# A hybrid decoder step on one Trainium2 core: filler matmuls moved inside the paged-attention rounds

## The chip, the cores and the metric

The kernel runs on one core of one Trainium2 chip. Its time is the device time of one execution in microseconds (us), the median of several executions. TensorE (PE) does the matmuls and the transposes, VectorE (DVE) and ScalarE (ACT) empty the PSUM banks and prepare operands, GpSimd (POOL) and SyncE (SP) mostly issue DMAs.

## The reference

Two trunk layers of a decoder are computed for a prompt group of 1024 tokens and for a sample group of 8 sequences with 4 new tokens each (1056 columns in all). The change touches only layer 0, and of it the part in which the sample group attends to its paged cache. In short:

```python
past_k = cache_k[j, page_table].reshape(nb, -1, DA_HEADS, 2 * DA_DIM)   # 8 sequences x 16 pages of 128 tokens
past_v = cache_v[j, page_table].reshape(nb, -1, DA_HEADS, 2 * DA_DIM)
...
proj = u @ w_in                                    # gate_b, gate_c, xin, q, k, v
conv_y, conv_new = short_conv(gate_c * xin, conv_w, conv_buf)
y_conv = gate_b * conv_y
...
s = einsum('bqhcd,bkhcd->bhcqk', q, keys) * (DA_DIM ** -0.5)
p = softmax(where(mask, s, -inf))
w = p[:, :, 0] - lam * p[:, :, 1]
attn = einsum('bhqk,bkhe->bqhe', w, vals)
mixed = concatenate([y_conv, rmsnorm(attn, subln_g) * (1 - lam_init)]) @ w_out
```

The convolution branch needs gate_c, xin and gate_b for 512 channels, that is 4 groups of 128 channels with three projections each.

## The kernel before

Every weight is split into a high and a low fp16 part, so a projection of 128 output channels (a *visit*) is computed as three products for each of the 8 slices of the input. A visit has three *units*, one for each third of the 1056 columns (352 columns, one PSUM bank). A unit is 24 matmuls of 128x352 (L369), and is issued in two *halves* of 12. The high part of a weight is made by ACT (L326), the low part by DVE (L342). A unit is drained from its bank by ACT (L1482) or by DVE (L1541 and L1545 for xin, L1560 for gate_b). In this stage nearly all of these units use the single bank 7, so a unit cannot start before the one ahead of it is drained.

The sample attention (`pe_samples`, `act_samples`, `dve_samples`) runs in two rounds of 4 sequences. A round consists of:

- the *K phase*, 32 steps. A step transposes two pages of K on PE (L1910, 8 transposes, banks 4 and 5), ACT copies one bank out (L1979) and DVE the other (L2039), and PE computes the scores of the step before (L1898). The transposes of a step wait until the banks of the step before are copied.
- the *middle*, 4 steps: own scores (L1917, L1921), maxima on DVE (L2034 to L2047), exponentials on ACT (L1985, L1987), the combination of the softmax on DVE (L2050 to L2053), and the transposed weights (PE L1927, L1929, L1934, copied by DVE L2056 and L2059 and ACT L1991).
- the *V phase*, 32 steps. A step multiplies two pages of V (L1949, 8 matmuls), and every eighth step adds the own rows (L1956).
- the *end*, 3 steps.

Pages of 256 KB lie in a ring of 16 (`ring`, in the rows of hT). The load of page f is issued once page f-16 has been used (semaphore `page_used`); of each four pages two are issued by SP and two by POOL (L1845). A page is waited for in pairs (`page_loaded`).

Between these steps PE, ACT, DVE and SP each weave in the 27 units of the three last visits of each kind (visits 15 to 23, units 45 to 71: gate_c, xin, gate_b of channel groups 1 to 3). `woven(chunk, fill, between)` takes one step of the attention and then as many half units as the table says; all four engines use the same table, SAMPLE_FILL. On SP a new weight panel of 512 KB is loaded with the first of every six halves (L284). The first unit of a gate_b visit also brings, on DVE, the taps of the convolution (L1507, L1508, then L1510, L1511, L1513, L1514), which stand ahead of the draining of that unit (L1560).

Of the kernel before, what the change touches and what calls it, by code (L numbers as in the profile page):

```python
# [77 lines left out]
def build(nc, x_p, x_s, cache_k, cache_v, state_conv, state_C, state_n, state_m, page_table, norms, w_in0,  # L78
# [3 lines left out]
    with ctx:  # L82
# [1749 lines left out]
            ins.then_inc(q_ready, 1)  # L1832


        ROUND_FILL = ((0,) * 32 + (2, 2, 2, 2) + (1, 0) * 15 + (0, 0) + (1, 1, 1))
        SAMPLE_FILL = (1, 1, 0) + ROUND_FILL * 2

        def load_page(eng, f):
# [1204 lines left out]
```

## Time and profile before

| | |
|---|---|
| median of 3 runs | 2750.39 us (2750.03 to 2756.36) |
| the profiled execution | 2750.39 us, span 2748.8 us |
| PE busy | 2648.7 us, 96% of the span |
| weight loads of PE | 1885.3 us, 69% |
| DVE, ACT, POOL busy | 1254.3 (46%), 1023.1 (37%), 445.2 us (16%) |
| chain that ended last | PE 89%, DVE 5%, ACT 3%, issue 2%, DMA 1% |
| mean granted TensorE clock | 0.989 |
| first K phase | 332.9 to 386.7 us |
| first V phase | 407.3 to 453.4 us |
| second K phase | 460.6 to 513.5 us |
| second V phase | 533.5 to 579.6 us |

The span is the profiler's time from the first to the last instruction. The chain of waits is followed back from the last instruction. Busy shares are means over stages that have different limits, so the stage that the change touches, about 325 to 600 us, is read by itself below.

### The profile page before, as it was taken

What the parts mean: (1) busy time and instruction counts of PE and PEld (TensorE: products, weight loads), DVE (VectorE), ACT (ScalarE), POOL (GpSimd) and SP (SyncE); (2) the same over time, 40 slices, a digit from 0 to 9 for tenths busy, and PEclk for the clock granted to TensorE, in tenths of its full rate; (3) what the DMA queues carried; (4) which work ended last, traced back from release to release, by engine and by line L of the source; (5) the groups of instructions that cost most, each with busy time, mean ns of one, the idle gap of its engine ahead of it and who ended that gap; (6) DMA issues with size and microseconds to landing.
All of it is one profiled execution on the core that took longest, in us unless ns stands there. A gap on an engine that the chain in (4) does not pass through costs nothing.

```text
span 2748.8 us, 49390 instructions
## 1 busy us (share of the span) xinstructions
PE 2648.7 (96%) x20145; PEld 1885.3 (69%) x20145; DVE 1254.3 (46%) x2087; ACT 1023.1 (37%) x1885; POOL 445.2 (16%) x500
## 2 busy tenths in 40 slices
PE   7999899999999999999999999999989999999997
PEld 5666566655688668876567676767646886788764
DVE  5555533435744214545753434344467541144444
ACT  4444432224444223434433232324355441244332
POOL 3000023222132002212201101010101220122121
PEclk8999999999999999999999999999999999999999
DMA  7111169771211301134334323222411121111442
GB/s 245 59 42 41 55 231 339 245 248 53 73 62 44 88 32 62 62 121 126 102 76 76 86 64 85 60 91 62 150 51 68 62 59 58 32 62 47 153 116 85
DMA packets 257516, 266.15 MB, mean 97 GB/s; under 512 B 10652, under 2 KB 217794, under 8 KB 256652
## 3 DMA queue, kind: packets, MB, share of 16 engines
q1 hardware_dynamic: 231772, 166.10, 21.7%
q0 software_dynamic: 24944, 94.79, 9.7%
q8 instruction: 162, 2.65, 0.4%
q10 hardware_dynamic: 576, 2.10, 0.2%
q14 instruction: 62, 0.51, 0.1%
HBM read 227.45 MB, written 35.50 MB: 96 GB/s over the span
## 4 chain that ended last, share of the span: by engine, by line
PE 89%; DVE 5%; ACT 3%; issue 2%; DMA 1%; POOL 0%; DVEq 0%; ACTq 0%; SPq 0%
PE ps L369 48%; PE ps L1106 24%; PE ps L1910 2%; PE ps L1596 1%; PE ps L1898 1%; PE ps L2470 1%; PE ps L1675 1%; PE ps L2461 1%; PE ps L1949 1%; PE ps L2439 1%; PE ps L2453 1%; PE ps L2419 1%; DVE arena L864 1%; DVE hT L868 1%; DVE w_split L342 1%
## 5 line engine op out<-in xcount | busy, mean ns | idle before, releaser
L369 PE MATMUL ps<-u,w_split 128*128 128x352 f16 (+1 forms) x4752 | 751.4, 314 | 7.6 <-DVE u L718 3.8
L369 PEld LDWEIGHTS ps<-u,w_split 128*128 128x128 f16 (+1 forms) x4752 | 460.9, 98 | 257.4 <-issue 22.6
L369 PE MATMUL ps<-arena,w_split 128*128 128x352 f16 x3663 | 561.3, 313 | 3.7 <-DVE w_split L342 1.5
L369 PEld LDWEIGHTS ps<-arena,w_split 128*128 128x128 f16 x3663 | 357.5, 98 | 201.4 <-issue 10.4
L1106 PE MATMUL ps<-hT,w_split 128*128 128x264 f16 x3456 | 400.6, 276 | 3.2 <-ACT arena L1146 3.2
L1106 PEld LDWEIGHTS ps<-hT,w_split 128*128 128x128 f16 x3456 | 337.8, 98 | 54.9 <-issue 2.1
L342 DVE SCALAR_TENSOR_TENSOR w_split<-w_raw,w_split 128x1024 f16<-128x1024 f32 (+2 forms) x133 | 184.5, 1389 | 306.3 <-ACT w_split L326 305.8
L1106 PE MATMUL ps<-u,w_split 128*128 128x264 f16 x2592 | 303.4, 276 | 0.0
L1106 PEld LDWEIGHTS ps<-u,w_split 128*128 128x128 f16 x2592 | 253.6, 98 | 38.3
L326 ACT ACTIVATE w_split<-w_raw 128x1024 f16<-128x1024 f32 (+2 forms) x133 | 155.6, 1172 | 148.4 <-PE ps L369 97.2
L340 DVE SCALAR_TENSOR_TENSOR w_split<-arena,w_split 128x512 f16<-128x512 f32 x126 | 85.9, 724 | 103.5 <-ACT w_split L320 103.5
L340 DVE SCALAR_TENSOR_TENSOR w_split<-w_raw,w_split 128x512 f16<-128x512 f32 x126 | 80.9, 687 | 62.4 <-ACT w_split L320 62.4
L1236 POOL TENSOR_TENSOR arena<-arena 128x512 f32<-128x512 f32 x18 | 22.8, 1265 | 526.9 <-DVE w_split L340 526.9
L2290 ACT ACTIVATE arena<-ps 128x352 f32<-128x352 f32 x66 | 30.5, 463 | 197.5 <-PE ps L369 197.4
L369 PE MATMUL ps<-arena 128*128 128x352 f16 x657 | 103.6, 318 | 0.0
L802 POOL TENSOR_TENSOR arena<-arena 128x352 f32<-128x352 f32 x54 | 75.6, 1400 | 171.4 <-ACT arena L790 171.2
L1179 DVE TENSOR_TENSOR arena<-ps,arena 128x528 f32<-128x528 f32 x36 | 25.5, 708 | 153.3 <-ACT arena L1146 153.3
L1276 ACT ACTIVATE arena<-ps 128x352 f32<-128x352 f32 x48 | 22.2, 463 | 191.4 <-PE ps L369 191.4
L369 PEld LDWEIGHTS ps<-arena 128*128 128x128 f16 x657 | 65.0, 99 | 38.2 <-issue 2.4
L1192 DVE TENSOR_TENSOR arena<-arena 128x1056 f16<-128x1056 f32 (+1 forms) x60 | 58.3, 971 | 50.4 <-ACT arena L1129 41.4
L369 PE MATMUL ps<-u,arena 128*128 128x352 f16 x504 | 77.5, 313 | 3.2 <-ACT arena L1274 2.7
L320 ACT ACTIVATE w_split<-arena 128x512 f16<-128x512 f32 x126 | 71.7, 619 | 13.7 <-PE ps L1106 10.9
(386 smaller groups left out, 3020.2 us busy)
## 6 DMA issues: line engine op xcount, KB each, us to landing
w_raw<-in_w_down SPq DMA_DIRECT2D x58, 704.0 KB, 4.8
w_raw<-in_w_in SPq DMA_DIRECT2D x56, 512.0 KB, 8.0
arena<-in_w_gu SPq DMA_DIRECT2D x18, 1024.0 KB, 5.2
w_raw<-in_w_gu SPq DMA_DIRECT2D x18, 1024.0 KB, 5.2
hT<-in_cache_k SPq DMA_DIRECT2D x64, 256.0 KB, 4.4
hT<-in_cache_k POOLq DMA_DIRECT2D x64, 256.0 KB, 4.7
hT<-in_cache_v SPq DMA_DIRECT2D x64, 256.0 KB, 5.1
hT<-in_cache_v POOLq DMA_DIRECT2D x64, 256.0 KB, 5.4
```

The lines of the kernel that those rows point to most:

```text
L320: act.activation(split_of(v, 0).rearrange("p (k n) -> p k n", k=kt), raw_of(v), ACT.Copy, scale=WS).then_inc(w_hi, 1)
L326: act.activation(split_of(v, 0)[:, 0:kt * n], raw_of(v), ACT.Copy, scale=WS).then_inc(w_hi, 1)
L340: dve.scalar_tensor_tensor(lo, raw_of(v), WS, hi, ALU.mult, ALU.subtract).then_inc(w_ready, 1)
L342: dve.scalar_tensor_tensor(split_of(v, 1)[:, 0:kt * n], raw_of(v), WS, split_of(v, 0)[:, 0:kt * n], ALU.mult, ALU.subtract).then_inc(w_rea ...
L369: ins = pe.matmul(ps[0:m, bank, 0:GW], split_of(v, wp)[:, k * w + col * P:k * w + col * P + m], x[:, xp, k0 + k, cols(g)], start=(k == 0 a ...
L802: pool.tensor_tensor(sum_y, sum_y, sq_y[k % 2], ALU.add).then_inc(y_added, 1)
L864: ins = dve.scalar_tensor_tensor(h_tmp[:, k % 2, :], ybuf[:, k, cols(g)], gains[:, col:col + 1], rs[0], ALU.mult, ALU.mult)
L868: dve.tensor_tensor(h, h, h_tmp, ALU.add).then_inc(h_ready, 1)
L1106: ins = pe.matmul(ps[:, bank + s_, 0:HW], split_of(v, wp)[:, k * P:(k + 1) * P], x, start=(name in ("M1", "M2", "M5") and k == 0 and q == ...
L1192: dve.tensor_tensor(hi_lo[:, 1], x, hi_lo[:, 0], ALU.subtract).then_inc(hid_ready, 1)
L1910: ins = pe.transpose(ps[:, 4 + e, h * P:(h + 1) * P], ring[:, f % RING, h * P:(h + 1) * P], ident[:, :])
L2290: act.activation((q_of[h % 2], k1, v1, o1)[m // 2][:, m % 2, cols(g)], ps[:, UNITS[n].bank, 0:GW], ACT.Sigmoid if m >= 6 else ACT.Copy, sc ...
```

## The change

Only the table of fillers changes. Of its 71 entries for one round the first 32 belong to the K phase, the next 4 to the middle, 32 to the V phase and 3 to the end. Both tables place 26 half units in a round.

```diff
-        ROUND_FILL = ((0,) * 32 + (2, 2, 2, 2) + (1, 0) * 15 + (0, 0) + (1, 1, 1))
+        ROUND_FILL = ((1, 0, 0, 0, 0, 0, 0, 0) * 4 + (2, 2, 2, 2) + (1, 0, 0) * 10 + (1, 0) + (1, 1, 1))
         SAMPLE_FILL = (1, 1, 0) + ROUND_FILL * 2
```

The K phase gets 4 halves (none before), the middle keeps 8, the V phase gets 11 (15 before), the end keeps 3. Since the halves follow one another in a fixed order, each place of the round now holds other units than before: of the first round, units 46 and 47 move from the middle into the K phase, and unit 51, the first of a gate_b visit, moves from the V phase into the end of the middle; of the second round, units 59 and 60 move into the K phase, and unit 60 is again the first of a gate_b visit.

PE at the start of the first K phase, before. L1910 are the page transposes (hT holds the ring), L1898 the scores, L369 half units.

```order
L1610 MATMUL ps<-ident,arena 128x128 x4
L1910 MATMUL ps<-ident,hT 128x128 x16
L1898 MATMUL ps<-arena 32x256 x4
L1910 MATMUL ps<-ident,hT 128x128 x8
L1898 MATMUL ps<-arena 32x256 x4
```

And now:

```order
L1610 MATMUL ps<-ident,arena 128x128 x4
L1910 MATMUL ps<-ident,hT 128x128 x8
L369 MATMUL ps<-u,w_split 128x352 x12
L1910 MATMUL ps<-ident,hT 128x128 x8
L1898 MATMUL ps<-arena 32x256 x4
```

A half unit stands behind the first step, and again behind steps 8, 16 and 24; the steps in between are as before.

PE from the end of the middle into the first V phase, before. L1934 are the last transposed weights, L1949 the products with the pages of V (8 a step).

```order
L1934 MATMUL ps<-arena 128x64 x8
L369 MATMUL ps<-u,w_split 128x352 x24
L1949 MATMUL ps<-hT,arena 4x128 x8
L369 MATMUL ps<-u,w_split 128x352 x12
L1949 MATMUL ps<-hT,arena 4x128 x16
L369 MATMUL ps<-u,w_split 128x352 x12
L1949 MATMUL ps<-hT,arena 4x128 x16
```

And now:

```order
L1934 MATMUL ps<-arena 128x64 x8
L369 MATMUL ps<-u,w_split 128x352 x24
L1949 MATMUL ps<-hT,arena 4x128 x8
L369 MATMUL ps<-u,w_split 128x352 x12
L1949 MATMUL ps<-hT,arena 4x128 x24
L369 MATMUL ps<-u,w_split 128x352 x12
L1949 MATMUL ps<-hT,arena 4x128 x24
```

Three steps of V instead of two now lie between half units. The unit of 24 matmuls behind L1934 was unit 49 and is now unit 51.

DVE in the middle of the first round, as a piece of the difference (- before, + now). L2050 to L2053 combine the softmax, L1541 drains xin units, L342 splits a weight.

```order
+L342 SCALAR_TENSOR_TENSOR w_split<-w_raw,w_split 128x1024
+L1536 COPY arena<-stT 128x8x2
+L1541 SCALAR_TENSOR_TENSOR arena<-ps,arena 128x352
 L2050 TENSOR_REDUCE small<-small 128x1
 L2051 RECIPROCAL small<-small 128x1
 L2052 TENSOR_TENSOR small<-small,part 128x1
 L2053 TENSOR_SCALAR arena<-pick,small 128x64
+L1541 SCALAR_TENSOR_TENSOR arena<-ps,arena 128x352
 L2056 COPY arena<-ps 32x64
-L342 SCALAR_TENSOR_TENSOR w_split<-w_raw,w_split 128x1024
-L1536 COPY arena<-stT 128x8x2
-L1541 SCALAR_TENSOR_TENSOR arena<-ps,arena 128x352
```

The draining of the xin units now stands ahead of and right behind the combination; the taps of unit 51 follow behind L2059, the last copy of the middle. In the second round the taps of unit 60 leave the middle and stand between page copies (L2039) of the K phase.

## Rows read from the trace of the kernel before

**Rows 1.** Busy time by stage: window, its length, then each engine, clock, DMA share, GB/s.
```profile
325.00:407.00 82.00, 74.90 (x695) 49.45 (x696) 34.17 (x60) 28.29 (x51) 17.25 (x32) 0.98 0.65 219
407.00:512.00 105.00, 103.23 (x1275) 64.84 (x1277) 38.56 (x68) 29.18 (x54) 33.28 (x62) 1.00 0.95 327
512.00:600.00 88.00, 82.91 (x1006) 53.05 (x999) 29.90 (x63) 20.22 (x44) 16.05 (x30) 1.00 0.70 242
```

**Rows 2.** Timeline of PE, first K phase: start, length, then idle time before and releaser.
```profile
332.86 3.50 PE L1910 MATMUL ps<-ident,hT 128*128 128x128 f32 x16 [1.83 <-issue]
...
336.86 1.09 PE L1910 MATMUL ps<-ident,hT 128*128 128x128 f32 x8
...
338.45 1.09 PE L1910 MATMUL ps<-ident,hT 128*128 128x128 f32 x8
```

**Rows 3.** Timeline of PE, middle and V phase of round 1.
```profile
386.72 3.75 PE L369 MATMUL ps<-u,w_split 128*128 128x352 f16 x24
391.12 3.74 PE L369 MATMUL ps<-u,w_split 128*128 128x352 f16 x24 [0.65 <-ACT arena L1482]
396.27 0.30 PE L1927 MATMUL ps<-arena 128*32 128x64 f32 x2 [1.41 <-DVE arena L2053]
...
403.65 3.74 PE L369 MATMUL ps<-u,w_split 128*128 128x352 f16 x24
407.32 0.62 PE L1949 MATMUL ps<-hT,arena 128*4 128x128 f32 x16
408.10 1.95 PE L369 MATMUL ps<-u,w_split 128*128 128x352 f16 x12 [0.16 <-DVE arena L1541]
409.98 1.06 PE L1949 MATMUL ps<-hT,arena 128*4 128x128 f32 x32
410.97 1.96 PE L369 MATMUL ps<-u,w_split 128*128 128x352 f16 x12
...
453.42 1.96 PE L369 MATMUL ps<-u,w_split 128*128 128x352 f16 x12
```

**Rows 4.** Timeline of PE, round 2.
```profile
462.00 1.16 PE L1910 MATMUL ps<-ident,hT 128*128 128x128 f32 x8 [0.34 <-ACT arena L1979]
...
518.06 3.74 PE L369 MATMUL ps<-u,w_split 128*128 128x352 f16 x24 [0.78 <-DVE arena L1545]
...
524.55 3.74 PE L369 MATMUL ps<-u,w_split 128*128 128x352 f16 x24 [0.59 <-DVE arena L1560]
```

**Rows 5.** Timeline of ACT, middle of round 1.
```profile
390.51 0.46 ACT L1482 ACTIVATE arena<-ps 128x352 f32<-128x352 f32 x1 [6.16 <-PE ps L369]
```

**Rows 6.** Timeline of DVE: page copy, exponentials' wait, last copy, taps.
```profile
341.18 0.69 DVE L2039 COPY arena<-ps 128x512 f32<-128x512 f32 x1 [0.90 <-PE ps L1910]
...
395.37 0.16 DVE L2050 TENSOR_REDUCE small<-small 128x1 f32<-128x5 f32 x1 [8.16 <-ACT arena L1987]
...
403.85 0.69 DVE L2059 COPY arena<-ps 128x512 f32<-128x512 f32 x1 [1.21 <-PE ps L1934]
...
518.70 1.22 DVE L342 SCALAR_TENSOR_TENSOR w_split<-w_raw,w_split 128x1024 f16<-128x1024 f32 x1
...
520.91 1.28 DVE L1510 SCALAR_TENSOR_TENSOR arena<-arena,gains 128x1024 f32<-128x1024 f32 x1
...
523.88 0.52 DVE L1560 SCALAR_TENSOR_TENSOR arena<-ps,arena 128x352 f32<-128x352 f32 x1
```

**Rows 7.** DMA, 424 to 453 us (V phase of round 1).
```profile
DMA packets 5515, 11.01 MB, mean 380 GB/s; under 512 B 648, under 2 KB 1672, under 8 KB 5509
```

**Rows 8.** Windows of K phase (first two) and V phase.
```profile
332.00:340.00 8.00, 7.14 (x56) 4.94 (x56) 3.03 (x5) 2.39 (x4) 1.37 (x3) 0.79 0.52 162
...
350.00:360.00 10.00, 10.00 (x103) 6.53 (x101) 4.15 (x6) 3.72 (x7) 3.22 (x6) 1.00 0.96 329
...
425.00:435.00 10.00, 10.00 (x173) 6.21 (x166) 3.18 (x5) 1.94 (x3) 3.23 (x6) 1.00 1.04 384
```

**Rows 9.** DMA, page loads: KB, median us to landing (350 to 370, then 555 to 565).
```profile
hT<-in_cache_k POOLq DMA_DIRECT2D x13, 256.0 KB, 4.7
...
hT<-in_cache_v SPq DMA_DIRECT2D x7, 256.0 KB, 7.2
```

**Rows 10.** Tile hT, 325 to 600 us: quickest, median and slowest load.
```profile
DMA to landing us min/median/max: 2.6/4.7/14.2
```

## Prediction

> **What bounds the kernel now.** I read the page first: PE is busy for 96% of the span and carries most of the chain of waits. Then the windows of the stage that the change touches [rows 1]: in 275 us (325 to 600) PE is busy for 261.0, so 14.0 us are idle, at a granted clock of 1.00 but for one dip. That is the ceiling of what any reordering can win here, and part of it has nothing to do with fillers. Then the timeline of PE [rows 2 to 4], to see where the idle time lies and what ends it, and last the DMA views [rows 7 to 10], since the ring of pages is the one resource that works near its limit: its share is 0.95 over 407 to 512 us [rows 1], 0.96 in the K phase and 1.04 in the V phase [rows 8].
>
> **The work that moves.** In each round four half units go from the V phase to the K phase. One costs PE 1.88 us between V steps (408.10 to 409.98) [rows 3]. In the K phase a step repeats every 1.59 us (336.86 to 338.45) without an idle gap [rows 2], so a half unit put there finds nothing to fill and costs the same 1.88. The eight halves are worth 0 as work. What is left are waits that vanish or appear.
>
> **Waits that shrink.**
> - Start of a K phase. The first 16 transposes wait for the copies of step 0; now a half unit stands between. In round 2 that wait is 0.34 [rows 4]; in round 1 most of the 3.50 us [rows 2] is half clock (0.79 over 8 us [rows 8]), which stays, and I take 0.3 for the wait. Gain 0.6.
> - Middle of round 1. PE waits 0.65, 1.41 and 0.16 [rows 3]. The 1.41 is the combination on DVE, which waited 8.16 us for the exponentials [rows 6], and these stood on ACT behind the draining of unit 46 at 390.51 [rows 5]. Now ACT has no unit to drain there (xin is DVE's), only a weight split that is done before the maxima are. So the exponentials start earlier, and the combination is finished while PE computes unit 49. Two units back to back in bank 7 still cost one drain, 0.7. The 0.16 is counted with the taps. Gain 0.65+1.41-0.7 = 1.4.
> - Middle of round 2. 0.78 and 0.59 [rows 4]; the second was the taps of unit 60, which are gone from there. One back-to-back drain of 0.65 stays. Gain 0.7.
>
> Together -2.7.
>
> **Waits that appear on DVE.** Unit 51 now stands in the last slot of the middle, and unit 52 follows after a single V step. DVE takes up unit 51 behind its copy L2059, which ends at 404.54, 0.89 us after the filler there starts (403.65) [rows 3, 6]. Split, taps and drain then take 518.70 to 524.40 = 5.70 us [rows 6], so bank 7 is free 6.6 us after the start of unit 51. PE wants it after 3.67 (403.65 to 407.32) and one V step of 0.62: 4.3 [rows 3]. PE stands for 2.3 us. Queued behind it on PE are all V steps, and behind these the page loads.
> In the second K phase the taps of unit 60 fall between page copies. At a step with a half unit, copies on DVE are 1.59+1.88 = 3.47 us apart, less 0.69 for the copy [rows 2, 3, 6] leaves 2.8. The first half asks for split and first tap, 518.70 to 520.91 = 2.2, plus about 0.5 for ACT's part of the split: hidden. The second asks for 520.91 to 524.40 = 3.5 [rows 6]: 0.7 over. Together +3.0. The bounds are 0 (I misplace the taps) and 4.5 (the first half overruns too).
>
> **The ring in the V phase.** This is the largest term. The V phase takes 46.1 us (407.32 to 453.42) with 15 halves [rows 3]; with 11 it would be 46.1-4x1.88 = 38.6 on PE alone. Its 64 pages are then wanted at 16.8 MB in 38.6 us = 435 GB/s, where the DMA engines, with a share of 1.04, moved 380 [rows 7, 8]. 16 pages lie ready at its start, so the question is when the others land. At 380 GB/s a page of 0.262 MB takes 0.69 us and a weight panel of 0.52 MB 1.38. Releases run freely from the second step on: 0.5 (step), 1.9 (half), 0.5 (step) and 0.6 for the issue, 3.5 us after the start of the phase. The pages of step 30 are the last behind which work remains (step 0.5, half 1.9, step 0.5, own rows 0.3: 3.2). Up to them 44 pages pass, and one panel in round 1, two in round 2. To this comes the delay of a load beyond its own transfer: 2.6-0.7 = 1.9 for the quickest [rows 10], 4.7-0.7 = 4.0 in the K phase [rows 9]; I take 2.8, between the two, since a part of the latter is waiting in the queue that I count already.
> Round 1: 3.5+2.3+30.4+1.4+2.8+3.2 = 43.6, against 38.6+2.3 = 40.9: stall 2.7.
> Round 2: 3.5+30.4+2.8+2.8+3.2 = 42.7, against 38.6: stall 4.1.
> Together +6.8. That this limit is near shows already: loads take 7.2 us at 555 to 565, against 4.7 in the K phase [rows 9]. With 1.9 for the delay it is 5.0, with 4.0 it is 9.2. If the engines could give more than they did, down to 0; this bound stays open, since no stretch asks for more. The K phases ask for less (4 halves more in the same 64 pages) and cannot run dry.
>
> **Sum.** 0-2.7+3.0+6.8 = +7.1. The profiled execution took 2750.39, which is also the median: 2757.5 us.
>
> **Rivals.**
> 1. *The ring keeps up.* If DMA delivers a page in 0.60 us, the sums above become 39.4 (round 1) and 38.3 (round 2), and no stall is left; it decides from 0.61 us a page (430 GB/s). Then -2.7+3.0 = +0.3: 2750.7, not slower. For it: PE never waited for a page, and the share of 1.04 was reached by demand, not by a queue without end. Against it: landing times that grow within the V phase.
> The Trainium skill (DMA: Bandwidth & Descriptors, section Bandwidth) gives 425 GB/s for a 16 MB transfer of a core alone, and 341 for 1 MB. By the first figure stalls of 0.5 us would be left and this rival would hold, by the second they would be larger than mine. The trace shows 380 in a saturated stretch [rows 7], and I go by it.
> 2. *Clock and copies.* After the idle pieces ahead of the first K phase the granted clock fell (0.79 over 8 us, 1.7 us lost) [rows 8]. The stand of 2.3 us before the second V step, beside V steps that stall one by one, may do so again, once or twice (+1.7 to 3.4), and the first taps may hold the copies too (+0.8), with the delay of a load at its upper bound (+2.4): 2750.4+7.1+1.7+0.8+2.4 = 2762.4.
> 3. *The waits go and nothing comes.* The taps are covered and the ring keeps up: -2.7, 2747.7. A gain larger than 0.3% would need 8.3 of the 14.0 idle us [rows 1], most of which lie at the ends of the rounds, which the table leaves alone.
>
> **Chances.** Forecast 0.60 (own range 2754 to 2761), ring keeps up 0.20, clock and copies 0.15, nothing comes 0.05. A measurement tells 0.3%, 8.3 us, from no change: the border of slower is 2758.6. Of the forecast about 0.4 lies above it (0.25), with rival 2 that makes 0.40 slower; faster by 8.3 us gets 0.03, the rest, 0.57, is the same. The range 2750 to 2764 takes in the rival at the lower side and most of the second at the upper.
>
> **What the profile will show.** Right: V phases of about 43.6 and 42.7 us instead of 46.1, DMA share about 1.04 through them, PE waiting for pages ("DMA" or "issue" ahead of L1949) in their second half; a wait of about 2.3 us for DVE L1560 after the first V step; no wait for L2053; K phases 7.5 us longer. Wrong: V phases of 38.6 and 41 us without gaps (rival 1), or a granted clock below 1.00 after 400 us (rival 2). The forecast fails outright if PE gets faster per step in the K phase, or if half units there cost less than 1.88 us each.

## The result, and the profile after

| | before | changed |
|---|---|---|
| median, five executions each, same chip | 2754.13 us (2750.03 to 2756.36) | 2767.31 us (2766.11 to 2769.72) |
| profiled execution | 2750.39 us, span 2748.8 | 2769.63 us, span 2768.0 |
| mean granted TensorE clock | 0.989 | 0.987 |

The ratio of changed to before is 1.0052, 95% interval 1.0041 to 1.0062: slower, by 13 us in the medians. The two profiled executions, the ones taken apart here, lie 19.2 us apart: that of before is near the lowest of its runs, that of the changed kernel near the highest of its own. The forecast was 2757.5 with a range up to 2764; the time lies above it. The mechanism named as the largest term, waits for pages in the V phases, is there, but at about twice its size (12.9 us against 6.8), and the granted clock, which the forecast left at full, fell as well.

The windows by stage of the changed kernel (columns as in rows 1):

```profile
325.00:407.00 82.00, 76.84 (x706) 50.13 (x707) 33.89 (x61) 28.79 (x52) 17.24 (x32) 0.98 0.68 219
407.00:512.00 105.00, 95.70 (x1169) 60.87 (x1167) 34.16 (x64) 24.55 (x46) 29.16 (x55) 0.97 0.85 289
512.00:600.00 88.00, 78.73 (x1008) 50.34 (x1005) 26.71 (x51) 18.87 (x42) 18.58 (x35) 0.96 0.70 231
```

Against [rows 1], the first stretch has PE busier by 2 us, the second less busy by 7.5 us at a clock of 0.97, the third by 4.2 us at 0.96. The loss begins in the first V phase; the K phase and the middle ahead of it gave something. What PE waited for, 400 to 605 us, by releaser (total us, times, longest):

```profile
PE ps L1949 <- DMA hT<-in_cache_v: 12.9, 9, 4.4
PE ps L369 <- DVE arena L1560: 3.8, 3, 2.4
```

The first row is new: in the kernel before PE never waited for a page of V. The timeline of PE through the first V phase, which runs from 412.2 to 461.9 us:

```profile
412.25 0.62 PE L1949 MATMUL ps<-hT,arena 128*4 128x128 f32 x16
...
438.77 0.62 PE L1949 MATMUL ps<-hT,arena 128*4 128x128 f32 x16 [1.14 <-DMA hT<-in_cache_v]
...
447.74 1.06 PE L1949 MATMUL ps<-hT,arena 128*4 128x128 f32 x32 [2.69 <-DMA hT<-in_cache_v]
...
450.75 1.03 PE L1949 MATMUL ps<-hT,arena 128*4 128x128 f32 x16 [1.63 <-DMA hT<-in_cache_v]
451.72 2.97 PE L369 MATMUL ps<-u,w_split 128*128 128x352 f16 x12
```

The waits come in the second half of the phase, where they were looked for. The last two rows show a second loss: after the two stands (a *stand* is a stretch in which PE waits with nothing to do) a half unit takes 2.97 us instead of 1.96, and 16 products take 1.03 us instead of 0.62. The windows there and at three other places:

```profile
416.00:420.00 4.00, 4.00 (x53) 2.26 (x54) 0.24 (x1) 0.00 (x0) 0.54 (x1) 0.57 0.15 52
450.00:454.00 4.00, 3.25 (x25) 1.68 (x26) 0.00 (x0) 0.00 (x0) 0.54 (x1) 0.57 1.04 387
573.00:580.00 7.00, 5.78 (x59) 2.98 (x60) 0.00 (x0) 0.00 (x0) 1.07 (x2) 0.52 1.02 360
607.00:611.00 4.00, 3.68 (x14) 1.91 (x15) 1.39 (x2) 0.00 (x0) 1.02 (x2) 0.57 0.65 233
```

Each window holds a stretch at 1.2 GHz, half of the full clock, where the granted clock is 1.00 in the two later stretches of [rows 1]; the one at 607 lies behind the stage. Each of the first three follows a stand of PE: 2.43 us for the taps, 2.69 and 1.63 for pages, 4.38 for pages. The third stands in the second V phase (548.4 to 596.5 us), here from the same timeline:

```profile
574.06 1.89 PE L1949 MATMUL ps<-hT,arena 128*4 128x128 f32 x32 [4.38 <-DMA hT<-in_cache_v]
```

During the longest wait the DMA engines were full. Their view of 564 to 574 us (packets, MB and share by queue; below, loads issued, KB, median us to landing):

```profile
DMA packets 1964, 3.77 MB, mean 377 GB/s; under 512 B 217, under 2 KB 838, under 8 KB 1964
...
q0 software_dynamic: 701, 2.30, 61.4%
q1 hardware_dynamic: 1263, 1.48, 43.3%
...
hT<-in_cache_v POOLq DMA_DIRECT2D x6, 256.0 KB, 6.4
hT<-in_cache_v SPq DMA_DIRECT2D x4, 256.0 KB, 11.2
```

377 GB/s is the rate that the prediction used (380) [rows 7]. But the bytes are not those that PE waits for: POOL's queue (q0) moved 2.30 MB and SP's (q1) 1.48, and a weight panel issued just before, at 558.67, stands in SP's queue too. POOL's pages land after 6.4 us, SP's after 11.2. Pairs of pages alternate between the two issuers, and PE uses them in order, so a late pair of SP stops it while POOL's later pairs arrive early. Sorting the page waits by the pair that PE then took, 10.2 us end with a pair of SP and 2.7 with one of POOL. The stand of 4.38 us shows it: it waits for page 33 of that round's V (counted from 0), which SP issued at 560.9 and which landed 13.0 us later; POOL's page 43, issued at 567.2, had landed before it. What SP was issuing in the first V phase (start of a row, length of the stretch, number of issues):

```profile
412.86 20.80 SPq L1845 DMA_DIRECT2D hT<-in_cache_v  x14
433.76 0.39 SPq L284 DMA_DIRECT2D w_raw<-in_w_in  x1
434.91 3.57 SPq L1845 DMA_DIRECT2D hT<-in_cache_v  x1
```

Most page issues take SP 0.34 us. Directly behind the panel of 433.76 one takes 3.57, and SP's pages issued from there on are those that PE stands for at 447.74 and 450.75, one ring later. The stand at 438.77 is older: SP had issued its pages at 429.8 and 431.1, ahead of the panel. In the second V phase the panel of 558.67 is followed by SP's loads of the pages that come late at 574.06; there the next issue took the usual 0.34 us, and only the landings were late.

Last, how fast the transfers get going, and what they do behind the long stand. Windows of the second V phase, from its start:

```profile
548.00:553.00 5.00, 4.91 (x84) 3.11 (x82) 0.00 (x0) 0.46 (x1) 0.54 (x1) 1.00 0.45 109
553.00:558.00 5.00, 5.00 (x86) 3.28 (x83) 1.40 (x2) 1.41 (x2) 2.25 (x5) 1.00 0.86 290
558.00:564.00 6.00, 6.00 (x120) 3.92 (x109) 0.53 (x1) 0.00 (x0) 2.85 (x6) 1.00 1.01 351
...
580.00:590.00 10.00, 10.00 (x187) 6.55 (x186) 5.44 (x11) 1.06 (x1) 3.22 (x6) 1.00 0.88 264
```

Against a steady 380 GB/s the first three lose 5x271/380 = 3.6, 5x90/380 = 1.2 and 6x29/380 = 0.5 us: 5.2 us of transfer time. The last one comes behind the stand of 4.38 us. While PE stood it freed no slots, and from 569.6 to 574.9 us no page load was issued at all; so there is less under way now, and 10x116/380 = 3.1 us are lost again. In the first V phase the taps' stand adds to that: the DMA share is 0.15 in 416 to 420.

**The account of the profiled executions.** A V phase is measured here from the start of the first product with V to the end of the last. Page waits 12.9 (5.9 in the first V phase, 7.0 in the second). Clock within the V phases 6.4, as what is left over: the first takes 49.6 us, the second 48.1, while PE alone needs 38.0 (measured below, run pages_half); 49.6-38.0-5.9-2.4 = 3.3 and 48.1-38.0-7.0 = 3.1. The three windows bear it out, 0.43x4+0.43x4+0.48x7 = 6.8, a part of it while PE stood. Taps 2.4, K copies 0.4, waits gone -2.5. Sum 19.6.

Two gains are missing in it. A half unit costs 1.96 us in the V phase (45.8 with 15 before, 38.0 with 11: 7.8/4) and 1.75 in the K phase (worked out under "The work that moves" below), so the eight give back 1.7. And the half-clock stretch that lay on the first transposes of K ([rows 2], 3.50 us for 16) falls ahead of a wait for DVE in the changed kernel, which saves about 1.5. That leaves 16.4 for the stage. The places of the same instructions in both traces say 16.3: PE is 0.9 us behind at 331 us and 17.2 behind at the end of the second round. The rest of the 19.2 lies outside: those 0.9, 1.6 for the stretch at 607, 0.4 later on.

### The profile page after: what moved, and what is told of

Read it like the earlier page. It is cut to its first block, busy times and chain, and to the rows that moved or that the text cites. A ratio compares the mean times of both kernels' runs of the same rounds, so it can differ in the third digit from the quotient of the medians.

```text
span 2768.0 us, 49389 instructions
## 1 busy us (share of the span) xinstructions
PE 2653.5 (96%) x20145; PEld 1887.2 (68%) x20145; DVE 1253.7 (45%) x2087; ACT 1023.3 (37%) x1885; POOL 445.4 (16%) x500
## 4 chain that ended last, share of the span: by engine, by line
PE 88%; DVE 5%; ACT 3%; issue 2%; DMA 2%; SPq 0%; POOL 0%; DVEq 0%; ACTq 0%
PE ps L369 47%; PE ps L1106 24%; PE ps L1910 2%; PE ps L1898 1%; PE ps L1596 1%; PE ps L2470 1%; PE ps L2461 1%; PE ps L1675 1%; DMA hT<-in_cache_v 1%; PE ps L2439 1%; PE ps L2453 1%; PE ps L2419 1%; DVE arena L864 1%; DVE hT L868 1%; PE ps L1949 1%
## 5 line engine op out<-in xcount | busy, mean ns | idle before, releaser
L369 PE MATMUL ps<-u,w_split 128*128 128x352 f16 (+1 forms) x4752 | 757.2, 316 | 9.2 <-DVE arena L1560 3.8
L369 PEld LDWEIGHTS ps<-u,w_split 128*128 128x128 f16 (+1 forms) x4752 | 463.1, 99 | 263.3 <-issue 25.2
L369 PE MATMUL ps<-arena,w_split 128*128 128x352 f16 x3663 | 563.0, 314 | 3.7 <-DVE w_split L342 1.5
L369 PEld LDWEIGHTS ps<-arena,w_split 128*128 128x128 f16 x3663 | 358.0, 98 | 202.5 <-issue 10.4
L342 DVE SCALAR_TENSOR_TENSOR w_split<-w_raw,w_split 128x1024 f16<-128x1024 f32 (+2 forms) x133 | 184.5, 1389 | 311.4 <-ACT w_split L326 310.9
L369 PE MATMUL ps<-arena 128*128 128x352 f16 x657 | 103.9, 318 | 0.0
L369 PEld LDWEIGHTS ps<-arena 128*128 128x128 f16 x657 | 65.0, 99 | 38.3 <-issue 2.4
L369 PE MATMUL ps<-u,arena 128*128 128x352 f16 x504 | 77.5, 313 | 3.2 <-ACT arena L1274 2.7
```

Of the source, the lines that this page charges most:

```text
L342: dve.scalar_tensor_tensor(split_of(v, 1)[:, 0:kt * n], raw_of(v), WS, split_of(v, 0)[:, 0:kt * n], ALU.mult, ALU.subtract).then_inc(w_rea ...
L369: ins = pe.matmul(ps[0:m, bank, 0:GW], split_of(v, wp)[:, k * w + col * P:k * w + col * P + m], x[:, xp, k0 + k, cols(g)], start=(k == 0 a ...
```

## The experiments

Each was timed beside the kernel before on the same chip. "Page waits" are PE's waits for V pages in 400 to 605 us of the profiled execution. They come from one execution each, so that a difference of one or two us between two kernels is weak evidence by itself; where the times agree with it is said at each run. Three runs also show waits with "issue" ahead of a product with V (1.3, 1.0 and 0.4 us). They lie inside a step, where no page is awaited, and the profile doesn't show their cause; they are not counted as page waits.

| run | ratio to before | 95% | V phases, us | page waits, us |
|---|---|---|---|---|
| before | 1 | | 45.8, 45.8 | 0 |
| changed kernel | 1.0052 | 1.0041 to 1.0062 | 49.6, 48.1 | 12.9 |
| panels_out | 1.0029 | 1.0019 to 1.0039 | 45.1, 42.0 | 5.9 |
| v_thin | 1.0073 | 1.0057 to 1.0090 | 46.7, 46.1 | 12.8 |
| half_dose | 1.0019 | 1.0009 to 1.0028 | 44.8, 43.1 | 2.7 |
| v_late | 1.0023 | 1.0014 to 1.0033 | 43.1, 42.4 | 8.6 |
| panel_rows | 1.0053 | 1.0036 to 1.0069 | 46.0, 45.5 | 9.4 |
| panels_act | 1.0041 | 1.0026 to 1.0056 | 46.3, 46.2 | 10.7 |
| late_out | 1.0002 | 0.9993 to 1.0011 | 40.8, 40.2 | 4.1 |
| pages_half | 0.9991 | 0.9981 to 1.0000 | 41.6, 38.0 | 0.2 |
| half_late_out | 1.0011 | 1.0002 to 1.0020 | 45.5, 41.6 | 2.0 |

### v_thin: the V phase thinned, nothing put into the K phase

```diff
-        ROUND_FILL = ((1, 0, 0, 0, 0, 0, 0, 0) * 4 + (2, 2, 2, 2) + (1, 0, 0) * 10 + (1, 0) + (1, 1, 1))
+        ROUND_FILL = ((0,) * 32 + (2, 2, 2, 2) + (1, 0, 0) * 10 + (1, 0) + (3, 2, 2))
```

> No half units in the K phases, 11 in each V phase as in the changed kernel, the four others at the end of the round (3, 2, 2). Ring theory: page waits of 10 to 14 us as in the changed kernel, no wait of 2.4 us for the taps behind the first V step, and a time 8 to 16 us above before. Rival (the K phase is what costs: copies of pages delayed by half units): page waits are gone or small and the time is that of before within 3 us.

Measured: 2772.3 us, against 2752.87 for before. The waits of its PE, 400 to 605 us:

```profile
PE ps L1949 <- DMA hT<-in_cache_v: 12.8, 10, 5.5
...
PE ps L369 <- DVE arena L1545: 1.5, 2, 0.8
PE ps L369 <- ACT arena L1482: 1.3, 2, 0.6
```

The page waits are those of the changed kernel, with no half unit in a K phase. Thinning the V phase is enough to bring them; the half units in the K phases are not their cause. The time is 19 us above before, more than the 8 to 16 expected, in part because units now stand back to back at the end of a round, each behind a drain (L1545, L1482), and because the taps of a gate_b unit hold PE for 2.60 us there.

### pages_half: the page loads halved

```diff
-            eng.dma_start(ring[:, f % RING, :], cache[0, ds(page, 1), :, :, :].rearrange("a t h e -> (a t) (h e)")
+            n = 2 if f // 64 % 2 else HEADS
+            eng.dma_start(ring[:, f % RING, 0:n * P].rearrange("p (a h e) -> p a h e", a=1, h=n),
+                          cache[0, ds(page, 1), :, 0:n, :].rearrange("a t h e -> t a h e")
```

> The changed kernel, but of each page of V only two of its four heads are loaded (128 KB instead of 256); PE multiplies all four as before, two of them with what lay in the ring, so the sample outputs differ. This takes the DMA limit away from the V phases and leaves everything else of the change. If the sum of the prediction is right but for its terms of the ring and of the clock, page waits are 0, the V phases take 38.6 us (41.0 in round 1 with the taps), no half clock but perhaps the one behind the taps' stand of 2.4 us, and the time is that of before within 3 us. If half units in the K phase or the other order of units cost by themselves, 4 us or more stay above before.

Measured: 2750.46 us against 2753.33, ratio 0.9991 (0.9981 to 1.0000). Waits of its PE, 325 to 605 us:

```profile
PE ps L1951 <- DMA hT<-in_cache_v: 0.2, 1, 0.2
```

With the order of instructions of the changed kernel and half the bytes of V, nothing of the 13 us is left. All other steps of the change together are within what can be told from nothing, as their terms say (-2.5+2.4+0.4, -1.7 for the work, up to +1.7 for the clock behind the taps). The second V phase gives PE's own time: 38.0 us; the forecast of 38.6 counted on to the start of the next half unit, 0.3 us more. The first still has the taps' stand and half clock behind it (41.6).

### panels_out: no weight panel among the loads of V pages

```diff
+        PANEL_AT = (0, 6, 12, 25, 26, 30, 36, 51, 52)
-            for v in range(v0, v1_ + 1):
-                load_tile(sp, v + 4)
-                for _ in range(6):
-                    yield
+            for n in range(6 * (v1_ + 1 - v0)):
+                for i, at_ in enumerate(PANEL_AT):
+                    if at_ == n:
+                        load_tile(sp, v0 + i + 4)
+                yield
```

> The changed kernel, with the weight panels that SP loads inside the V phases issued behind them instead (nothing else moves). In the changed kernel PE waits 12.9 us for pages of V. Theory Q (queues): SP's and POOL's queue share the DMA engines about equally, a panel of 512 KB in rows of 512 bytes holds SP's queue for 4 to 5 us, and PE waits for SP's pairs while POOL's pages lie ready. Then the waits for pages fall below 5 us and the time by 8 us or more (with the clock that the long stands cost). Theory B (bytes): only the sum of bytes at 380 GB/s counts, a panel is worth 1.4 us. Then the waits fall by about 4, to 9 us, and the time by 4.

Measured: 2761.1 us against 2752.87. Waits of its PE, 400 to 605 us (lines are three higher than in the changed kernel: L1952 is the product with V):

```profile
PE ps L1952 <- DMA hT<-in_cache_v: 5.9, 5, 2.4
...
PE ps L1952 <- issue: 1.3, 2, 1.0
```

The larger of the two "issue" waits, in PE's timeline; it stands behind the sixth product instruction of a step:

```profile
451.17 1.03 PE L1952 MATMUL ps<-hT,arena 128*4 128x128 f32 x26 [0.95 <-issue]
```

12.9 us of page waits become 5.9: 7.0 come from the four panels that were moved. In the changed kernel they are issued at 433.8, 462.3, 558.7 and 586.4, and only two of them stand among SP's pages of V: that of 462.3 comes behind the V phase, and that of 586.4 behind SP's last page (585.5), where it can only share the engines with POOL's last ones. The formula counted three panels, at 1.4 each: 4.1. That was one too many in round 2; the two that stand there are worth 2.8 by it. The time falls by five to six of the 13 us (2761.1-2752.87 = 8.2 are left), between the two theories. Without panels the formula gives 1.3 in each round (43.6-1.4-40.9 and 42.7-2.8-38.6), 2.6 in all; 5.9 is measured. So of the 6.1 us by which the term was missed, 3.3 are there with no panel among the pages at all.

### panel_rows: the same panels, in long rows

```diff
+            if l in (22, 23, 26, 27):
+                sp.dma_start(dst, w_in0[0, 0:P, 0:k * n]).then_inc(w_loaded[which], 16)
+                return
```

> The changed kernel, but the four weight panels that SP loads during the V phases come from contiguous rows of 4 KB (the first 128 rows of w_in0) instead of rows of 512 bytes; the same 512 KB, the same place in SP's queue. What is left out: visits 22, 23, 26 and 27 compute with these other weights, so the numbers differ. Theory Q1 (it is the small rows that hold SP's queue): the page waits fall from 12.9 us to near those without panels (6 to 8), and the two long stands of 2.7 and 4.4 us go; time 4 to 7 us below the changed kernel. Theory Q2 (any 512 KB ahead of pages in that queue): page waits stay at 11 to 13 us and the time stays.

Measured: 2765.6 us against 2751.2. Page waits 9.4:

```profile
PE ps L1952 <- DMA hT<-in_cache_v: 9.4, 7, 2.7
...
PE ps L1952 <- issue: 1.0, 1, 1.0
```

In this profile the page waits are 3.5 us lower with long rows. In time the run is not told apart from the changed kernel (1.0036 to 1.0069 against 1.0041 to 1.0062). Neither theory is borne out, and the run is inconclusive on the row length.

### panels_act: the same panels on ACT's queue

```diff
-                load_tile(sp, v + 4)
+                if v + 4 not in (22, 23, 26, 27):
+                    load_tile(sp, v + 4)
+        def act_panels(act, units_):
+            for n, _ in enumerate(units_):
+                if n in (18, 24, 42, 48):
+                    load_tile(act, CXB + 7 + n // 6)
+                yield
...
-            woven(act_samples(act), act_proj0(act, CXB + 3, WO0 - 1), SAMPLE_FILL)
+            woven(act_samples(act), act_panels(act, act_proj0(act, CXB + 3, WO0 - 1)), SAMPLE_FILL)
```

> The changed kernel, with the same four panels issued by ACT at the same half units instead of by SP: the same bytes and the same small rows in the same stretch, but not ahead of SP's pages in their queue. Theory Q (order in SP's queue): the page waits fall to 6 to 9 us, since a third queue takes its share from both others evenly, and the time falls by 4 to 7 us. Theory B (bytes or rows in the engines): page waits stay near 12.9 us.

Measured: 2763.08 us against 2751.2, page waits 10.7. Loads issued from 425 to 445 us:

```profile
hT<-in_cache_v POOLq DMA_DIRECT2D x15, 256.0 KB, 6.3
hT<-in_cache_v SPq DMA_DIRECT2D x15, 256.0 KB, 8.6
w_raw<-in_w_in ACTq DMA_DIRECT2D x1, 512.0 KB, 18.8
```

The panel itself now lands after 18.8 us, and the page waits fall by 2.2 us: those that end with SP's pairs from 10.2 to 6.4, while those that end with POOL's rise from 2.7 to 4.2. SP's pages are still later than POOL's, 8.6 against 6.3. So in this profile the place in SP's queue is a part of what the panels cost (about 2.2 of 7.0), not all: the transfer itself, wherever it is queued, is the larger part. In time the run is not told apart from the changed kernel either (1.0026 to 1.0056), so the split stays open.

### half_dose: two half units a round in the K phase

```diff
-        ROUND_FILL = ((1, 0, 0, 0, 0, 0, 0, 0) * 4 + (2, 2, 2, 2) + (1, 0, 0) * 10 + (1, 0) + (1, 1, 1))
+        ROUND_FILL = ((1, 0, 0, 0, 0, 0, 0, 0, 0, 0, 0, 0, 0, 0, 0, 0) * 2 + (2, 2, 2, 2) + (1, 0) * 8 + (1, 0, 0) * 5 + (0,) + (1, 1, 1))
```

> Half the change: 2 half units in a K phase, 13 in a V phase. The V phase then wants its 64 pages in 42.3 us, 397 GB/s. Theory B: 1 us of stall in each round, time 0 to +3 us over before. Theory Q: 2 to 3 us in each round, +4 to +7. A linear rule (half of the measured 13) gives +6.5. The granted clock should stay at 1.00 in the V phases, since no stand is over 2 us.

Measured: 2757.84 us against 2752.87. Page waits are down to 2.7, in six pieces of at most 0.7, as theory B has them, but the time is 5 us above before, as theory Q has it:

```profile
PE ps L1949 <- DMA hT<-in_cache_v: 2.7, 6, 0.7
```

The second price is the taps. With two halves in the K phase the first unit of a gate_b visit falls into the middle of the second round, and PE stands 2.50 us for it there, from its timeline:

```profile
524.89 3.74 PE L369 MATMUL ps<-u,w_split 128*128 128x352 f16 x24 [2.50 <-DVE arena L1560]
```

Each change of the table moves these taps somewhere; that is a term of its own, and it does not follow the DMA. So the time here can't tell B from Q. The granted clock stayed at 1.00 behind this stand.

### v_late: the sparse part of the V phase put first

```diff
-        ROUND_FILL = ((1, 0, 0, 0, 0, 0, 0, 0) * 4 + (2, 2, 2, 2) + (1, 0, 0) * 10 + (1, 0) + (1, 1, 1))
+        ROUND_FILL = ((1, 0, 0, 0, 0, 0, 0, 0) * 4 + (2, 2, 2, 2) + (0,) * 4 + (1, 0, 1, 0, 0) * 5 + (1, 0, 0) + (1, 1, 1))
```

> The changed kernel, but the first half unit of a V phase stands behind step 4 instead of step 0 and the 11 are packed into the 28 steps left. Theory T (taps and clock): the stand of 2.4 us for the taps before the second V step falls to under 0.5, the half-clock stretch behind it goes (1.7 us), and the time is 3 to 5 us below the changed kernel. Theory G (given back): the V phase ends when its last pages land, so the page waits grow by what the taps' wait gave up, and the time is that of the changed kernel within 1 us.

Measured: 2759.43 us against 2752.87 (its profiled execution 2755.63). Waits of its PE, 400 to 605 us, and windows over most of its two V phases:

```profile
PE ps L1949 <- DMA hT<-in_cache_v: 8.6, 6, 3.4
```

```profile
412.00:453.00 41.00, 36.05 (x631) 23.04 (x630) 7.33 (x12) 4.77 (x8) 14.49 (x27) 1.00 1.01 360
540.00:580.00 40.00, 35.59 (x597) 22.51 (x598) 8.03 (x15) 2.93 (x4) 13.05 (x24) 1.00 0.94 330
```

Here the first V steps run without half units, so the slots come free early, and the taps are done by the time PE wants unit 52 but for 0.7 us. Compared with the changed kernel the DMA share is 1.01 instead of 0.90 (412 to 462), the taps' stand of 2.4 us is gone, the clock stays at 1.00, and the page waits fall by 4.3, against theory G. In the second V phase, where no taps stand in either kernel, they fall from 7.0 to 4.4. The first V phase is 6.5 us shorter, with the same number of half units in it. The time is 1.0023 of before instead of 1.0052, more than theory T had. The two panels among the pages now come two to three steps later as well, so this run alone doesn't show that it is the early slots; late_out against panels_out does, where no panel stands among the pages in either: 4.1 us of page waits against 5.9, and 1.0002 of the time of before against 1.0029.

### late_out: both together

The edits of v_late and panels_out in one kernel.

> Both remedies on the changed kernel: first half unit of a V phase behind step 4, and no panel inside a V phase. By the sum of the single runs (12.9 us of page waits, less 6.7 for the panels, less 4.2 for the late start) 1 to 3 us of page waits are left, no stand for the taps in the first V phase and no half clock there. Then the time is that of before within 3 us (-2.7 of waits gone, +0.4 for the copies, +1 to 3 of pages). Rival: the remedies act on the same microseconds, page waits stay at 5 us or more, time 4 us or more above before.

Measured: 2751.53 us against 2751.2, ratio 1.0002 (0.9993 to 1.0011). Waits of its PE and windows over its V phases:

```profile
PE ps L1952 <- DMA hT<-in_cache_v: 4.1, 6, 1.8
```

```profile
412.00:453.00 41.00, 38.06 (x671) 24.52 (x669) 8.34 (x13) 4.77 (x8) 15.56 (x29) 1.00 0.99 355
540.00:580.00 40.00, 38.06 (x672) 24.18 (x664) 9.08 (x17) 3.31 (x5) 12.88 (x24) 1.00 0.97 343
```

The whole loss is gone, with the half units of the changed kernel still in the K phases. What is won in the middles is given back in the 4.1 us of page waits that stay, above the 1 to 3 expected and all of them for SP's pairs. It is no faster than before, and no run was by more than the noise.

### half_late_out: fewer half units moved, late start, no panels

```diff
-        ROUND_FILL = ((1, 0, 0, 0, 0, 0, 0, 0) * 4 + (2, 2, 2, 2) + (1, 0, 0) * 10 + (1, 0) + (1, 1, 1))
+        ROUND_FILL = ((1, 0, 0, 0, 0, 0, 0, 0, 0, 0, 0, 0, 0, 0, 0, 0) * 2 + (2, 2, 2, 2) + (0,) * 4 + (1, 0) * 12 + (1, 0, 0, 0) + (1, 1, 1))
```

The edit is made to the changed kernel, with PANEL_AT as in panels_out.

> Half the dose (2 half units in a K phase, 13 in a V phase), the first of a V phase behind step 4, no panels inside V phases. Page waits 0 to 1 us, V phases of 42.3 us. Of the waits of the middle the 1.4 us for the combination stays, that of 0.3 at the start of a K phase goes. Time: before, or 1 us less; if it is not below before, a V phase that is fed in time gains nothing, since the K phases have nothing to hide behind a half unit.

Measured: 2757.07 us against 2753.33, ratio 1.0011 (1.0002 to 1.0020). Waits of its PE, 400 to 605 us:

```profile
PE ps L369 <- DVE arena L1560: 3.2, 2, 2.5
PE ps L1952 <- DMA hT<-in_cache_v: 2.0, 1, 2.0
```

Only one page wait is left, of 2.0 us, but the granted clock fell behind it, to a mean of 0.96 in that V phase, which took 45.5 us where 42.3 were expected. The taps cost 2.5 in the middle of the second round, as in half_dose, and here the clock fell behind them too. The expectation (0 to 1 us of page waits, time as before or 1 us less) was missed: the time is 0.1% above before. Less moved is not better than late_out.

## Why the prediction was wrong, point by point

**The work that moves: nearly right, and 1.7 us the other way.** The forecast took 1.88 us for a half unit in both places, and 0 for the eight. From the timeline of the changed kernel:

```profile
349.13 1.96 PE L369 MATMUL ps<-u,w_split 128*128 128x352 f16 x12
350.93 1.04 PE L1910 MATMUL ps<-ident,hT 128*128 128x128 f32 x8
```

350.93-349.13 = 1.80 us, and the transposes behind it take 1.04 instead of 1.09, so 1.75. In the V phase the 1.88 leaves out that products run closer together without a half unit between them: two steps and a half unit repeat after 2.87 us (408.10 to 410.97 [rows 3]), three steps and a half unit after 3.32 (420.22 to 423.54 in the changed kernel). So a step is 0.45 and a half unit 1.97. Moving eight gains 8x(1.96-1.75) = 1.7 us. The prediction called a half unit under 1.88 in the K phase a sign that it fails outright; that sign came, but it makes the changed kernel faster, and is no part of the loss.

**Waits that shrink: right**, -2.5 against -2.7 (0.65+1.41+0.16+0.34+0.78+0.59 before, twice 0.71 now). The combination L2053 is no longer waited for, because the exponentials no longer stand behind a drain on ACT; in each middle one drain stays, as forecast at 0.7 and 0.65:

```profile
393.07 3.75 PE L369 MATMUL ps<-u,w_split 128*128 128x352 f16 x24
397.53 3.74 PE L369 MATMUL ps<-u,w_split 128*128 128x352 f16 x24 [0.71 <-DVE arena L1541]
...
533.67 3.74 PE L369 MATMUL ps<-u,w_split 128*128 128x352 f16 x24 [0.71 <-DVE arena L1560]
```

**Waits that appear on DVE: right**, 2.43 and 0.37 us against 2.3 and 0.7:

```profile
415.30 2.79 PE L369 MATMUL ps<-u,w_split 128*128 128x352 f16 x12 [2.43 <-DVE arena L1560]
...
518.05 0.63 PE L1910 MATMUL ps<-ident,hT 128*128 128x128 f32 x4 [0.37 <-DVE arena L2039]
```

**The ring in the V phase: the step that failed.** That PE would wait for pages was right, and rival 1 (a ring that keeps up) is refuted, by the page waits and by pages_half. The size was not: +6.8 forecast, 12.9 measured, above the upper bound of 9.2. The formula took the 16 DMA engines as one line that is full from 3.5 us on at 380 GB/s and serves the pages in the order in which PE wants them. The rate while PE stood was right (377). Three things were not:
- It is not one line. SP's and POOL's queues share the engines without regard to what PE needs first: in the worst stretch 43.3% and 61.4%, with landings of 11.2 and 6.4 us. 10.2 us of the waits end with SP's pairs. In late_out, which moves all eight half units too and has the shortest page waits of such runs, all 4.1 us do.
- It is not full throughout. The prediction expected a DMA share of 1.04 through the V phases; the means are 0.90 (412 to 462) and 0.84 (548 to 597 us). The start costs 5.2 us of transfer in the second V phase; the formula has 3.5 for it and 2.8 more for the delay of a load, which may cover the difference. But a stand frees no slots, and behind that of 4.38 us another 3.1 us of transfer are lost (264 GB/s in 580 to 590), for which the formula has nothing. Sooner slots help: v_late has 4.3 us less of page waits, late_out 1.8 less than panels_out.
- The panels cost 7.0 us, not 4.1, and only two of the three counted stand among the pages. How the 7.0 divide is open: one profile each puts about 2.2 on their place ahead of SP's pages (panels_act) and up to 3.5 on their short rows (panel_rows), and neither shows in the time.

The Trainium skill (DMA: Bandwidth & Descriptors, section Bandwidth) was weighed in the prediction with 425 GB/s, by which no ring stall worth a term was left. The trace shows no such rate in the full stretches read, but 377 and 387 GB/s at shares of 1.05 and 1.04, so for this mix the measurement decides against it.

**The clock: the second miss.** The forecast put it at 0 and left it to rival 2, with 1.7 us for one dip; it is about 6.4 us in the V phases. Rival 2 came to 2762.4, the nearest of the four to the result, and its condition came true. Of its terms the clock was too small, the taps' +0.8 did not come, and the +2.4 for a longer landing delay was less than the waits grew by. Every half-clock stretch within a V phase, in all these runs, stands behind a stand of PE. The reverse doesn't hold (last section), and no run changed the clock alone, so that the stands cause it is read from the rows and not shown.

**The range.** Its upper end took one dip and the upper bound of the landing delay. A wait that comes true can lower the clock as well, so these two are not independent: the larger the stalls, the larger both.

**Left open.** Of the 5.9 us of page waits without panels among the pages 2.6 are the formula's; the rest, 3.3, is put down to the order of the two queues and to slots that come late, which were not isolated. Nor is it shown why SP's pages are the late ones when no panel stands among them. A ring in which single pages alternate between the queues would tell; it wasn't tried.

## What to carry to other kernels

When work is thinned out of a phase fed by a nearly saturated ring (here a share of 1.04), the phase may not get shorter by that work but wait, and here the price was more than bytes over rate: look at how soon the first slots are released, which queue each piece comes through, and what else stands in that queue. Put the sparse steps of such a phase first and keep other transfers out of it: the two together undid the loss here (1.0052 to 1.0002). Price a stand together with the clock that may fall behind it (1.7 us a stretch here), and follow heavy rare work such as these taps to its new slot with every table.

## What was not expected of the hardware

- Behind a panel of 512 KB the next DMA issue of SP took 3.57 us instead of 0.34 (434.91 us in the changed kernel). In v_late it took 3.30 and 3.19 behind both panels; behind that of 558.67 in the changed kernel it took 0.34. So the issuing engine can be held by what it issued before, and the runs don't show when.
- Page loads of equal size landed after 6.4 us from POOL's queue and 11.2 from SP's, at the same time. The Trainium skill (DMA: Bandwidth & Descriptors, section Issuing engines are not separate DMA queues) says that transfers run on the same 16 engines in the end and interleave whoever started them. The traces agree that they share the rate, and show that the order between queues still matters: a panel moved to ACT's queue landed after 18.8 us, instead of 12.5 on SP's (14.3 and 12.0 in the second round).
- The same stand of 2.43 us for the taps, at the same place, was followed by half clock in the changed kernel and in pages_half, and not in panels_out. PE's row and the window behind it in panels_out, and the window in pages_half:

```profile
415.91 1.95 PE L369 MATMUL ps<-u,w_split 128*128 128x352 f16 x12 [2.43 <-DVE arena L1560]
```

```profile
414.00:420.00 6.00, 4.09 (x66) 2.82 (x67) 2.25 (x4) 0.50 (x1) 0.54 (x1) 1.00 0.47 119
```

```profile
415.00:419.00 4.00, 4.00 (x32) 2.09 (x36) 0.53 (x1) 0.37 (x1) 0.00 (x0) 0.57 0.06 22
```

A longer stand passed without it as well: in v_late PE stood 3.39 us for a page, in a V phase whose clock is 1.00 throughout (its window above).

```profile
445.05 0.62 PE L1949 MATMUL ps<-hT,arena 128*4 128x128 f32 x16 [3.39 <-DMA hT<-in_cache_v]
```

Nor does it take a stand this long: in half_late_out the clock fell behind one of 2.04 us, and in v_thin during the last of three of 0.44, 1.17 and 0.95 us (577.8 to 584.0 us). A stand is thus a risk of some 1.7 us on top of itself, not a certainty.
